# Two-layer hybrid decoder trunk on one core: where the attention outputs of layer 0 are divided by their softmax sums

## What is computed

```python
logits = jnp.where(valid, logits, -jnp.inf)
p = jax.nn.softmax(logits, axis=-1)
o = jnp.einsum('bqgrk,bqkgd->bqgrd', p.astype(vsel.dtype), vsel)
...
mix = jnp.concatenate([o_a.astype(x.dtype), o_b], axis=-1) @ even_w_out[j]
```

## Time and profile before

| what | value |
|---|---|
| median of 3 runs | 2714.78 us (2711.61 to 2716.91) |
| the profiled execution | 2711.42 us |
| its span | 2709.7 us |
| TensorE busy | 2499.4 us, 92% |
| VectorE busy | 1616.1 us, 60% |
| ScalarE busy | 1051.9 us, 39% |
| GpSimd busy | 1280.0 us, 47% |
| mean granted TensorE clock | 0.955 |

### The profile page before, as it was taken

How to read it: one execution, slowest core, us unless ns; L and a number is a source line. 1 busy time by engine, 2 the same in 40 slices (tenths; PEclk the granted TensorE clock), 3 DMA queues, 4 the chain that set the end, 5 groups by cost and what they waited for, 6 DMA issues and landing times.

```text
span 2709.7 us, 31273 instructions
## 1 busy us (share of the span) xinstructions
PE 2499.4 (92%) x11133; PEld 1985.0 (73%) x11133; DVE 1616.1 (60%) x2354; ACT 1051.9 (39%) x1741; POOL 1280.0 (47%) x674
## 2 busy tenths in 40 slices
PE   6899798799778899999999989989988999999999
PEld 4677676355777688888888877766677888888887
DVE  6478568984886454445554755666444446544483
ACT  4255687556443433222232145435443222322220
POOL 4201233676763265556665712125515466655591
PEclk7999898799899899999999999988999999999999
DMA  4211123000300211112210222202002122111211
GB/s 148 51 28 28 32 67 91 15 8 13 117 16 1 63 55 39 34 58 62 62 46 24 70 98 55 63 16 74 24 19 60 47 62 62 54 37 33 62 62 62
DMA packets 164002, 136.57 MB, mean 50 GB/s; under 512 B 22969, under 2 KB 137730, under 8 KB 163906
## 3 DMA queue, kind: packets, MB, share of 16 engines
q1 hardware_dynamic: 152658, 124.58, 15.3%
q10 hardware_dynamic: 11248, 10.75, 1.5%
HBM read 116.17 MB, written 13.63 MB: 48 GB/s over the span
## 4 chain that ended last, share of the span: by engine, by line
PE 73%; DVE 10%; issue 8%; ACT 4%; POOL 2%; DMA 0%; ACTq 0%; DVEq 0%; POOLq 0%
PE ps L2150 22%; PE ps L2151 21%; PE ps L2152 21%; ACT signs L1218 1%; PE ps L2345 1%; PE ps L2504 1%; POOL cl L892 1%; PE ps L2262 1%; PE ps L2353 1%; DVE ub L2043 1%; DVE QL L1785 1%; PE ps L2333 1%; DVE ps L1723 1%; POOL w_lo L723 1%; DVE ps L1804 1%
## 5 line engine op out<-in xcount | busy, mean ns | idle before, releaser
L2150 PE MATMUL ps<-h_hi,w_hi 128*128 128x512 f32 x1680 | 670.8, 399 | 13.6 <-POOL w_lo L741 9.7
L2151 PE MATMUL ps<-h_lo,w_hi 128*128 128x512 f32 x1680 | 659.8, 393 | 0.0
L2152 PE MATMUL ps<-h_hi,w_lo 128*128 128x512 f32 x1680 | 659.4, 392 | 0.0
L2150 PEld LDWEIGHTS ps<-h_hi,w_hi 128*128 128x128 f32 x1680 | 319.4, 190 | 83.2 <-issue 14.4
L723 POOL TENSOR_TENSOR w_lo<-w_raw,w_hi 128x1024 fp32r<-128x1024 f32 x73 | 193.4, 2650 | 381.9 <-ACT w_hi L1228 376.9
L2151 PEld LDWEIGHTS ps<-h_lo,w_hi 128*128 128x128 f32 x1680 | 319.6, 190 | 67.8 <-issue 3.9
L2152 PEld LDWEIGHTS ps<-h_hi,w_lo 128*128 128x128 f32 x1680 | 318.9, 190 | 68.0
L2040 DVE TENSOR_TENSOR x_res<-ps,x_res 128x1024 f32<-128x1024 f32 x224 | 268.9, 1221 | 115.4 <-PE ps L2152 115.4
L2021 DVE TENSOR_TENSOR u_all<-ps,u_all 128x512 f32<-128x512 f32 x112 | 77.4, 691 | 416.0 <-ACT u_all L1125 416.0
L741 POOL TENSOR_TENSOR w_lo<-w_raw,w_hi 128x1024 fp32r<-128x1024 f32 x112 | 267.1, 2402 | 104.4 <-ACT w_hi L1114 104.4
L2150 PE MATMUL ps<-w_hi,uo_hi 128*128 128x512 f32 x784 | 307.5, 392 | 3.0 <-DVE shared L2040 3.0
(11 more groups left out here) (349 smaller groups left out, 4519.9 us busy)
## 6 DMA issues: line engine op xcount, KB each, us to landing
w_raw<-in_mlp_w_up SPq DMA_DIRECT2D x64, 512.0 KB, 4.0
w_raw<-in_mlp_w_down SPq DMA_DIRECT2D x64, 512.0 KB, 3.8
w_raw<-in_even_w_in SPq DMA_DIRECT2D x23, 512.0 KB, 3.7
x_res<-in_x SPq DMA_DIRECT2D x16, 512.0 KB, 8.8
w_raw<-in_odd_w_in SPq DMA_DIRECT2D x10, 512.0 KB, 3.6
scr_x<-x_res SPq DMA_DIRECT2D x8, 512.0 KB, 2.6
x_res<-scr_x SPq DMA_DIRECT2D x8, 512.0 KB, 4.3
out<-x_res SPq DMA_DIRECT2D x8, 512.0 KB, 2.6
```

The costliest lines, as they stand in the source:

```text
L2150: t_.matmul(out_, ah, bh, start=first, stop=False)
L2151: t_.matmul(out_, ah, bl, start=False, stop=False)
L2152: return t_.matmul(out_, al, bh, start=False, stop=last)
```

## The change

The division of blocks 0 to 6 in layer 0 is taken from steps 4, 8, 14, 22, 32, 44, 58 and put in steps 44, 48, 52, 57, 60, 63, 66. The rounding by ScalarE and the low part by GpSimd go with it, two steps behind: steps 46, 50, 54, 59, 62, 65, 68 in place of 6, 10, 16, 24, 34, 46, 60. Nothing is added or removed, no DMA is touched, and layer 1 and block 7 stay as they are.

```diff
@@ -499,6 +499,9 @@
         ROUND = (LAG + 3, LAG + 4)
         STEPS = [len(TILES[l]) + ROUND[l] + 1 for l in range(2)]
 
+
+        DIVIDED = {44: 0, 48: 1, 52: 2, 57: 3, 60: 4, 63: 5, 66: 6}
+
         OC_FIRST, OC_SUMS, OC_TILES = 8, 16, (4, 5, 6, 7, 0, 1, 2, 3)
@@ -534,6 +537,13 @@
+        def rounded_at(layer, n):
+
+            if layer == 0:
+                return DIVIDED.get(n - 2)
+            u = ends_at(layer, n - ROUND[layer])
+            return u // 2 if u is not None and u % 2 else None
@@ -865,9 +875,8 @@
-                    u = ends_at(layer, n - ROUND[layer])
-                    if u is not None and u % 2 and (layer or u // 2 < T - 1):
-                        q = u // 2
+                    q = rounded_at(layer, n)
+                    if q is not None:
                         dst = block_outputs(layer, q)
                         pool.wait_ge(att["o_hi"], Z["o_hi"] + q + 1)
@@ -1885,11 +1893,10 @@
                     u = ends_at(layer, n - LAG - 1)
-                    if u is not None and u % 2:
-                        if layer == 1:
-                            invert_sums(u // 2)
-                        elif u // 2 < T - 1:
-                            normalise(u // 2)
+                    if u is not None and u % 2 and layer == 1:
+                        invert_sums(u // 2)
+                    if layer == 0 and n in DIVIDED:
+                        normalise(DIVIDED[n])
```

## The result

| what | before | changed |
|---|---|---|
| median | 2715.23 us (2710.19 to 2720.62, 6 runs) | 2701.2 us (2697.89 to 2703.29, 6 runs) |
| the profiled execution | 2711.42 us | 2702.92 us |
| its span | 2709.7 us | 2701.2 us |
| mean granted TensorE clock | 0.955 | 0.956 |

The ratio is 0.9948, with a 95% interval of 0.9933 to 0.9963: 14.0 us faster, between 10 and 18. The prediction said 10.2 us, which is 2704.6 us from its median; that its 2701.2 us for the profiled execution equals the measured median is chance, for that execution took 2702.92. The pair of profiled executions is only 8.5 us apart, and most of the experiments are about this difference between 8.5 and 14.

The account below looks back on a forecast made before the run. It took layer 0's attention to be bound by VectorE first, then mixed, then by TensorE; 7.4 + 1.05 + 0.88 + 1.4 - 0.5 = 10.2 us took the median of 2714.78 to 2704.6 us, range 2699 to 2712.

Parts of the forecast that it names:

- as worked out: The main case for the whole kernel: a gain of 7 to 13 us, chance 0.62.
- more from the clock: Rival: low clock stretches at the begin of blocks 3 to 5 go too, 4.2 us more, 2700.4 us; chance 0.08.
- Block 0: Division at step 4: VectorE gains 1.8 us, then waits for rounded queries; TensorE gains 0.6 us.
- Block 1: Division at step 8: tile 12 starts 1.7 us earlier, `QL` 3.4 us; VectorE waits for ScalarE's query rounding.
- Block 2: Division at step 14: all 3.99 us count, maximum 7.4 us earlier, TensorE's 5.31 us wait falls to 1.3.
- Blocks 3 and 4: Divisions at steps 22 and 32: one TensorE wait for VectorE goes behind each, 1.05 and 0.88 us.
- The clock: TensorE's low-clock stretch behind its 5.31 us wait stays high instead: 1.4 us gained.
- the sign that was named: TensorE's granted clock at 1.00 for the 5 us behind the former 5.31 us wait.
- The new places: Steps 44 to 55: 0.5 us lost through GpSimd's late diagonal of step 49; from step 57 on nothing.
- GpSimd as the bound: Rival: all seven `h_lo` are paid in the TensorE-bound part, 9.0 to 22.8 us, up to 2727.4 us; chance 0.04.
- The block boundaries take more: Rival: tile 12 moves only by ScalarE's 0.6 us, gain 3 to 7 us, 2709 to 2710 us; chance 0.18.
- Port sharing: Rule against: seven moved VectorE products contend with GpSimd's `PL` and `h_lo`, up to 4.8 us lost if nothing hid it.

Follow-up runs that it names:

- e5: The kernel before, unchanged, profiled a second time; its attention took 193.66 us.
- e11: The changed kernel, unchanged, profiled once more; this execution took 2697.63 us, its attention 177.52 us.
- e3: The kernel before with only the divisions of blocks 3 to 6 moved, to steps 57, 60, 63 and 66; 2708.71 us, ratio 0.9975.
- e6: The kernel before with only the divisions of blocks 3 and 4 moved, to steps 48 and 52; 2710.96 us, ratio 0.9985.
- e7: The changed kernel without the reciprocal and product of blocks 0 to 6, one element copied instead; attention 184.70 us against 185.16.
- e12: The changed kernel with ScalarE's query rounding and copy ahead of the signs, and divisions in steps 44, 50, 57, 59, 61, 63, 66; 2695.58 us, ratio 0.9934.
- e8: The changed kernel with ScalarE rounding the next queries and issuing their copy before the signs at a block's first tile; 2697.11 us, ratio 0.9931.
- e9: The kernel before with ScalarE rounding the next queries and issuing their copy before the signs at a block's first tile; 2714.47 us, ratio 1.0004.

## Why the prediction was right, step by step

The time, 2701.2 us, lies in the range, and what was to be seen in the traces is there: the stretch that VectorE bounded got shorter by about the forecast amount. The size by the medians was 14 to 15 us and not 10.2. By the prediction's own cases that is not "as worked out" (7 to 13 us) but "more from the clock" (13 to 17), which had 0.08. That the range held it is in part luck. By pieces of the attention (us gained):

| piece | forecast | before to changed | e5 to changed | before to e11 |
|---|---|---|---|---|
| tiles 0 to 20 | 7.4 + 1.4 = 8.8 | 9.3 | 8.1 | 12.5 |
| tiles 20 to 42 | 1.05 + 0.88 = 1.9 | 0.8 | -0.4 | 5.2 |
| tiles 42 to 71 | -0.5 | -0.7 | 0.7 | -0.7 |
| sum | 10.2 | 9.3 | 8.5 | 17.0 |

The columns differ by more than most terms of the sum. So where a bullet below says "right", it means the first pair of traces.

- **Block 0.** Said: VectorE 1.8 us, TensorE 0.6. Measured from the attention's start: `QL` 1.8 us earlier (28.98 against 30.77), tile 7 0.5. Right, though e5 has tile 7 another 1.6 us earlier than the first trace of before.
- **Block 1.** Said: tile 12 1.7 us, `QL` 3.4. Measured: 2.15 and 3.7. Right, and the idle time of VectorE ahead of both `QL` is there. Of its first 8.0 us VectorE turned some 4 into waits, as worked out.
- **Block 2.** Said: the maximum 7.4 us earlier, 1.3 us of TensorE's wait left, and "the bound holds". Measured: 8.5 us, none left, and the bound did not hold. 0.3 of the 8.5 came with `QL`. Most of the rest is one instruction of `choose_keys` ahead of the scan (L1765, now L1773), which took 1.67 us before and 0.81 now; before, GpSimd's `PL` ran beside it, and that this is the cause is argued. TensorE was to reach the place 3.4 us earlier and reached it only 1.3 us earlier within the attention (the diagonal matmul ahead of it starts at 531.76 us, before at 534.60). It came from the copy wait of 1.89 us through a low stretch of the clock, and VectorE waited 1.33 us for it. The wait of 2.61 us for `PL` that the prediction overlooked lies on TensorE's way to the same place.
- **Blocks 3 and 4.** Said: the two waits of 1.05 and 0.88 us, together 1.9. The waits went. But the time between tiles 20 and 42, against 57.57 and 56.43 us before, was 56.8 in three executions and 52.36 in a fourth, and 53.7 and 53.8 in e3 and e6. The gain is between -0.4 and 5.2 us, and it follows the clock; at an equal clock of 0.97 it is 2.7 us. This is one of the two terms that were mis-sized.
- **The clock.** Said: 1.4 us, for one low stretch that would go. It went, and others grew in its place. Changed kernel, the stretches behind the copy wait of 1.89 us, at the place in question, and behind the copy wait of 2.65 us:

```profile
524.00:530.00 6.00, 5.73 (x14) 3.72 (x15) 5.86 (x12) 3.04 (x6) 3.66 (x7) 0.50 0.00 0
531.00:547.00 16.00, 14.33 (x56) 8.22 (x56) 12.74 (x31) 9.63 (x17) 11.09 (x12) 1.00 0.05 11
548.00:554.00 6.00, 6.00 (x14) 3.93 (x15) 5.86 (x12) 2.72 (x5) 3.52 (x7) 0.50 0.00 0
```

The middle one is the sign that was named. But before, the low stretches at the same block beginnings lasted about 3 us each (526 to 529 and 560 to 563) and not 6 to 7. In three executions of the changed kernel the pieces have as much low clock as before (0.78 and 0.91 against 0.79 and 0.94), so it gave nothing there, and the fourth was 7.7 us shorter at once. The step that failed is to have read the low stretches of one execution as a property of the kernel, and this is the other mis-sized term. The rival that the clock gives more had 0.08 and describes e11 in the main: the low stretches behind the copy waits of blocks 4 and 5 went although the waits stayed. That of block 3 stayed, 3 us long.
- **The new places.** Said: 0.5 us in tiles 50 to 55 and nothing later. Measured: 0.46 (e7). Right, with its place, and TensorE had no wait for `PL` there.
- **GpSimd as the bound.** It didn't come true with a division every third step. e12, with one every second step, shows its price: GpSimd's 0.60 us of idle time per tile don't cover an `h_lo` of 1.28 us in two tiles, and 1.1 us is lost from tile 60 on. The bound is real, and small.
- **The block boundaries take more.** Not so: tile 12 moved as far as the small waits allowed. That they are the next bound is what e8 and e9 point to.
- **Port sharing.** VectorE's products do meet GpSimd in the new places. One row each, before in rows 10, after here (ns min/median/max):

```profile
L882 POOL TENSOR_TENSOR h_lo<-o_den,h_hi x15: 1267/1278/1736, 610.7 to 1968.9; 128x512 fp32r<-128x512 f32 x15
...
L1847 DVE TENSOR_TENSOR o_den<-o_sum,o_den x7: 692/882/1741, 608.5 to 648.6; 128x512 f32<-128x512 f32 x7
```

The product went from a median of 0.69 to 0.88 us and a maximum of 1.74. In most meetings here it was VectorE that waited, which had nothing else to do from step 57 on, so the rule, by which up to 4.8 us could have gone, cost nothing visible: all that the divisions cost here is e7's 0.46 us.

What remains open is how the medians come to 14 to 15 us. The profiled executions give 8.4 to 9.3 us in the attention for three of the changed kernel and 16 to 17 for the fourth. If all executions are mixtures of such cases, 14 to 15 us on average is natural. The times fit this: the two profiled executions among the twelve timed ones of the changed kernel, 2705.17 and 2702.92 us, are the slowest and the third slowest of them, while e11, the one with the high clock, took 2697.63. But how often each case comes was not measured, since the clock inside the attention is only known for the profiled executions. That part is argued, not shown.

## What to carry to other kernels

A step that nobody reads soon should not stand in the order of the engine that bounds its stretch, even if the engine is at 60% over the program; look for a later stretch with another bound, and check the engine behind it in order (here GpSimd, with its diagonal and its low parts) for room. Price such a move by what is late next at each point: half of the first 8 us of VectorE's time that were freed turned into waits for ScalarE, and an edit of ScalarE's order that was worth nothing before was worth some 2 to 4 us afterwards by the medians. And where the clock changes level within the stretch, profile the same kernel a second time before reading a term off one trace, and compare pieces that ran at the same clock.

## What the runs showed of the hardware

- The granted clock in the same stretch of the same program was 0.91 in one execution and 1.00 in another, with the same waits of TensorE for a DMA (2.67 and 2.69 us at step 22). The two differ by 4.4 of 56.8 us there and by 7.7 of 185 over the attention, more than half of what the whole change is worth.
- 28 us of VectorE, divisions of 3.34 us and products, cost 0.46 us when they lie beside a stretch that TensorE bounds.
- A VectorE product of two SBUF operands, 0.69 us alone, took up to 1.74 us beside GpSimd's low parts, and a pair of these 2.97 us and not 2.56 in e12: each side can be the one that is stretched.
- The same VectorE scan of 128x768 took 2.82 us in two executions and 1.75 us in two others with the same order of work up to there, and the wait of TensorE behind it 5.3 against 3.1 and 3.5 us. The cause is open.
